# Attention value transposes one slot earlier, the last pair's stages a quarter unit later, and the last two down units with the final norm by token halves

## What is computed

```python
hn = rmsnorm(h, norm1)
q, k, v, g, ... = hn @ W_in                      # one combined projection
a = retention(4 heads);  b = gated_linear_attention(4 heads)
c = band_softmax_attention(8 heads)              # own chunk and 8 before
h = h + concat[a, b, c] @ W_out
h = h + relu(rmsnorm(h, norm2) @ W_up)**2 @ W_down
...
y = rmsnorm(h, final_norm)                       # after the second layer
```

## Time and profile before

| | us |
|---|---|
| median of 3 runs | 1369.89 (1369.73 to 1370.03) |
| profiled execution | 1369.59 |
| its span, first to last instruction | 1367.8 |
| TensorE busy in the span | 1338.8 (98%) |
| VectorE, ScalarE, GpSimd busy | 970.7, 644.5, 118.6 |
| mean granted TensorE clock | 0.994 of full speed |

### The profile page before, as it was taken

The page is one execution under the profiler, slowest core; times in us unless marked ns, Lnnn a source line. Parts: engine busy times, 40 slices in busy tenths (PEclk is TensorE's granted clock), DMA queues, the critical chain, the costliest instruction groups (busy, mean ns, idle before and its releaser), DMA issues. The chain is left out here.

```text
span 1367.8 us, 28726 instructions
## 1 busy us (share of the span) xinstructions
PE 1338.8 (98%) x12206; PEld 1296.8 (95%) x12206; DVE 970.7 (71%) x1480; ACT 644.5 (47%) x1051; POOL 118.6 (9%) x93
## 2 busy tenths in 40 slices
PE   9999999999999999999999999999999999999996
PEld 8999889899999999999998999888999999999995
DVE  6897766778767567666759967767885776756753
ACT  5423555746526337255433345566572462542741
POOL 0000000012020110200200000000211102011011
PEclk9999999999999999999999999999999999999997
DMA  6223333222222223223221223431222232222311
GB/s 232 70 67 102 100 101 120 79 85 86 99 102 78 97 90 108 80 91 109 84 74 49 69 86 124 130 104 63 93 87 100 78 109 93 88 98 93 96 60 66
DMA packets 50639, 127.83 MB, mean 93 GB/s; under 512 B 8400, under 2 KB 17744, under 8 KB 50512
## 3 DMA queue, kind: packets, MB, share of 16 engines
q1 hardware_dynamic: 50224, 125.44, 27.5%
q10 hardware_dynamic: 288, 0.55, 0.1%
HBM read 118.77 MB, written 7.21 MB: 92 GB/s over the span
## 5 line engine op out<-in xcount | busy, mean ns | idle before, releaser
L1685 PE MATMUL PS<-zhi,wlo 128*128 128x272 f32 x1280 | 370.4, 289 | 0.0
L1685 PE MATMUL PS<-zhi,whi 128*128 128x272 f32 x1280 | 368.8, 288 | 0.4 <-DVE wlo L984 0.4
L1685 PE MATMUL PS<-zlo,whi 128*128 128x272 f32 x1280 | 368.3, 288 | 0.0
L539 ACT ACTIVATE whi<-raw 128x1024 fp32r<-128x1024 f32 x136 | 143.7, 1058 | 308.8 <-PE PS L1685 303.9
L1685 PE MATMUL PS<-xhi,whi 128*128 128x272 f32 x896 | 268.9, 300 | 2.3 <-DVE wlo L984 2.2
L1685 PE MATMUL PS<-xhi,wlo 128*128 128x272 f32 x896 | 258.9, 289 | 0.0
L1685 PE MATMUL PS<-xlo,whi 128*128 128x272 f32 x896 | 258.5, 289 | 0.0
L1685 PEld LDWEIGHTS PS<-zhi,whi 128*128 128x128 f32 x1280 | 241.0, 188 | 0.9 <-DVE wlo L984 0.9
L1685 PEld LDWEIGHTS PS<-zlo,whi 128*128 128x128 f32 x1280 | 241.2, 188 | 0.0
L1685 PEld LDWEIGHTS PS<-zhi,wlo 128*128 128x128 f32 x1280 | 240.6, 188 | 0.0
L984 DVE TENSOR_TENSOR wlo<-raw,whi 128x1024 fp32r<-128x1024 f32 x136 | 209.3, 1539 | 39.9 <-ACT whi L539 39.0
(11 more groups left out here) (287 smaller groups left out, 2427.8 us busy)
## 6 DMA issues: line engine op xcount, KB each, us to landing
raw<-in_wu SPq DMA_DIRECT2D x199, 512.0 KB, 3.5
Bh<-in_bias SPq DMA_DIRECT2D x16, 256.0 KB, 4.0
h<-in_x SPq DMA_DIRECT2D x8, 272.0 KB, 6.2
out_k_t<-att_k SPq DMA_DIRECT2D x8, 272.0 KB, 4.4
out_y_t<-y SPq DMA_DIRECT2D x8, 272.0 KB, 2.7
kct<-in_ck SPq DMA_DIRECT2D x8, 256.0 KB, 3.3
cvb<-in_cv SPq DMA_DIRECT2D x8, 256.0 KB, 4.0
out_v_p<-vtk SPq DMA_DIRECT2D x8, 256.0 KB, 2.2
```

The source lines that it names most:

```text
L539: nc.scalar.activation(whi[n % SPL][:, :], raw[n % RAW][:, :], ACT.Copy).then_inc(sems["w_hi"], 1)
L1685: return nc.tensor.matmul(out, lhsT, rhs, start=start, stop=stop, skip_group_check=True)
```

## The change

Three parts.

1. `heads` of pairs 1 to 3 moves from slot (16+3u, 1) to (15+3u, 1), behind `turn_s` of the pair in front. It writes PSUM banks `M0 + 1` and `M0 + 2` where it wrote `M0` and `M0 + 2`.
2. The last pair: TensorE takes `turn 1` ahead of (27, 1), where it took it in the middle of (27, 0), and `pv` and `turn_s` in the middle of (27, 1), where it took them ahead of it. ScalarE's copies of `turn 1` move from slot (27, 0) to (27, 1), and with that behind `gate_out(1)` and `gate_log(2)`; its and VectorE's `pv` steps go behind the last slot's gate work.
3. The end: `d6` and `d7` run as first half of `d6`, first half of `d7`, second half of `d6`, second half of `d7`. VectorE scales and adds both by halves (GpSimd no longer takes part in `d6` and `y`). The norm's sums, root, broadcast and `y` are made for each token half: those of the first half stand on TensorE between the matmuls of the second. The outputs go in eight DMAs of two tiles x 272 tokens; two of the last four are issued by ScalarE's queue.

```diff
-    PE_STEPS[(_b, 1)] = [("heads", _u)]
+    if _u == 0:
+        PE_STEPS[(_b, 1)] = [("heads", _u)]
...
-    PE_STEPS[(_b + 2, 1)] = [("pv", _u), ("turn_s", _u)]
-
-MID = [("back", GLA), ("back", RET), ("turn", 3, 1)]
+    PE_STEPS[(_b + 2, 1)] = [("pv", _u), ("turn_s", _u)] + [("heads", _u + 1)] * (_u < 3)
+
+PE_STEPS[(27, 0)], PE_STEPS[(27, 1)] = [], [("turn", 3, 1), ("pv", 3), ("turn_s", 3)]
+MID = [("back", GLA), ("back", RET), ("pv", 3), ("turn_s", 3)]
...
+ACT_STEPS[(27, 1)], DVE_STEPS[(27, 1)] = [("turn", 3, 1)], []
...
                         if half == 1 and n > GATE:
                             gate_exp(n - GATE - 1)
+                    stage(("pv", 3))
+                    stage(("turn_s", 3))
...
-                for m in range(KC):
-                    if m < YP:
-                        sp.wait_ge(y_pool, m + 1)
-                    else:
-                        sp.wait_ge(y_dve, m - YP + 1)
-                    sp.dma_start(y_t[m, :, :], y[m][:, :]).then_inc(y_out, 16)
+                for a in range(2):
+                    c = slice(a * HT, (a + 1) * HT)
+                    for m in range(0, KC, 2 + 2 * a):
+                        sp.wait_ge(y_dve, a * KC + m + 2)
+                        sp.dma_start(y_t[m:m + 2, :, c].rearrange("m p t -> p m t"), y[:, m:m + 2, c]).then_inc(y_out, 16)
...
+                for a in range(2):
+                    c, o = slice(a * HT, (a + 1) * HT), slice(a * YT, (a + 1) * YT)
+                    for i in range(2):
+                        act.wait_ge(tail_added, 2 * a + i + 1)
+                        squares(KC - 2 + i, L, c)
...
+                for m in (2, 6):
+                    act.wait_ge(y_dve, KC + m + 2)
+                    act.dma_start(y_t[m:m + 2, :, HT:T].rearrange("m p t -> p m t"), y[:, m:m + 2, HT:T]).then_inc(y_out, 16)
...
+                tail_add(0, 0)
+                tail_add(1, 0)
+                tail_square(0)
+                tail_rstd(0)
+                tail_add(0, 1)
+                tail_square(1)
+                tail_y(0, range(6))
+                tail_add(1, 1)
+                tail_y(0, range(6, KC))
+                tail_rstd(1)
+                tail_y(1, range(KC))
...
+                def tail_sums(a):
+
+                    pe.wait_ge(sems["ss_ready"], L * KC + KC - 1 + a)
+                    pe.wait_ge(sems["squared"], L * 2 * KC + KC + 2 * a)
+                    for i in range(YT):
+                        t0, o = a * HT + min(i * P, HT - P), PS[:, M0, a * YT + i:a * YT + i + 1]
+                        mm(o, ssum[:, t0:t0 + P], ones[:, 0:1], True, False)
+                        last = mm(o, nt[1][:, t0:t0 + P], ones[:, 0:1], False, True)
+                    last.then_inc(y_sums, 1)
...
+                begin(d6)
+                tail_products(d6, 0)
+                begin(d7)
+                tail_products(d7, 0)
+                tail_products(d6, 1, all_kc[:4])
+                tail_sums(0)
+                tail_products(d6, 1, all_kc[4:])
+                tail_wide(0)
+                tail_products(d7, 1)
+                tail_sums(1)
+                tail_wide(1)
```

More of the change, by code:

```diff
@@ L34 @@
 NEG = -1e30
-YP = 2
+YT = 3
 WARM = 16
@@ L245, in hybrid_encoder @@
         sm = sb("sm", [P, L * NSM + KC])
-        yv, yl, yr, yn = (sb(n, [P, NT + 1]) for n in ("yv", "yl", "yr", "yn"))
+        yv, yl, yr, yn = (sb(n, [P, 2 * YT]) for n in ("yv", "yl", "yr", "yn"))
         dec = sb("dec", [P, 2, NC + 1])
@@ L312, in hybrid_encoder @@
         assert o + 32 * HT <= nc.sbuf_usable_end
-        y = [at(f"y{m}", [P, T], arena + 4 * T * m) for m in range(KC)]
-        y_rstd = at("y_rstd", [P, T], arena + 4 * T * KC)
+        y = at("y", [P, KC, T], arena)
         PS = ctx.enter_context(nc.psum_tensor("PS", [P, 8, 512], F32))
-        y_by = [PS[:, b:b + 2, :].rearrange("p a b -> p (a b)")[:, 0:T] for b in (M0 + 2, 0)]
         def halves(t):
@@ L333, in hybrid_encoder @@
         x_in = [sem(f"x_in{kc}") for kc in range(KC)]
-        y_sums, y_mean, y_log, y_guess, y_col, y_wide, y_copied, y_scaled, y_dve, y_pool, y_out = (
-            sem(n) for n in ("y_sums", "y_mean", "y_log", "y_guess", "y_col", "y_wide", "y_copied", "y_scaled",
-                             "y_dve", "y_pool", "y_out"))
+        tail_done, tail_added, y_sums, y_mean, y_log, y_guess, y_col, y_wide, y_dve, y_out = (
+            sem(n) for n in ("tail_done", "tail_added", "y_sums", "y_mean", "y_log", "y_guess", "y_col", "y_wide",
+                             "y_dve", "y_out"))
         names = [
@@ L500, in _ @@
                         for m in range(KC):
-                            if g == GROUPS - 1 and m == KC - 1:
+                            if g == GROUPS - 1 and m == KC - (1 if layer + 1 < L else 2):
                                 break
@@ L505, in _ @@
                                 .then_inc(sems["sq_used"], 1)
[L507 to L510, removed]
             @block.scalar
@@ L657, in stage @@
                             s = u % 2
-                            nc.scalar.activation(vtk[s][:, 0:NT, :], PS[:, M0, :].rearrange("p (i c) -> p i c", c=P), ACT.Copy)
+                            nc.scalar.activation(vtk[s][:, 0:NT, :], PS[:, M0 + 1, :].rearrange("p (i c) -> p i c", c=P), ACT.Copy)
                             nc.scalar.activation(vtk[s][0:TS, NT, :], PS[0:TS, M0 + 2, 0:P], ACT.Copy) \
@@ L952, in _ @@
                         next_x(KC - 1)
[L953 to L963, removed]
+                for a in range(2):
[3 more added lines that the diff above has]
+                        squares(KC - 2 + i, L, c)
+                    act.wait_ge(y_mean, a + 1)
+                    nc.scalar.activation(yl[:, o], yv[:, o], ACT.Ln).then_inc(y_log, 1)
+                    act.wait_ge(y_log, a + 1)
+                    nc.scalar.activation(yr[:, o], yl[:, o], ACT.Exp, scale=-0.5).then_inc(y_guess, 1)
+                for m in (2, 6):
+                    act.wait_ge(y_dve, KC + m + 2)
+                    act.dma_start(y_t[m:m + 2, :, HT:T].rearrange("m p t -> p m t"), y[:, m:m + 2, HT:T]).then_inc(y_out, 16)
             @block.vector
@@ L1609, in _ @@
                         for m in range(1, KC):
-                            scaled(m - 1, g)
+                            if m < KC - 1 or g < GROUPS - 1 or layer + 1 < L:
+                                scaled(m - 1, g)
                             if m < KC - 1:
@@ L1636, in _ @@
                         xlo_tile(KC - 2, w0 + NSM, 2 * KC - 1)
-                    add_square(KC - 2, layer + 1)
-                    last_scaled()
-                    if layer + 1 < L:
+                        add_square(KC - 2, layer + 1)
+                        last_scaled()
                         rest(UNITS + 1)
@@ L1642, in _ @@
                         add_square(KC - 1, layer + 1)
-                for a in range(2):
-                    c = slice(a * HT, (a + 1) * HT)
[L1646 to L1661, removed]
+                def tail_add(i, a):
+                    m, c = KC - 2 + i, slice(a * HT, (a + 1) * HT)
+                    dve.wait_ge(tail_done, 2 * a + i + 1)
+                    dve.wait_ge(sems["sq_used"], nth("sq_used", GROUPS * KC + m - 1))
+                    link(nc.vector.tensor_tensor(sq[i][:, c], PS[:, bank(m) + a, 0:HT], r2[:, c], ALU.mult))
+                    nc.vector.tensor_tensor(h[:, m, c], h[:, m, c], sq[i][:, c], ALU.add).then_inc(tail_added, 1)
@@ new lines, in tail_square, with tail_rstd @@
+                def tail_square(a):
+                    c = slice(a * HT, (a + 1) * HT)
+                    dve.wait_ge(sems["squared"], L * 2 * KC + KC - 1 + 2 * a)
+                    dve.wait_ge(sems["ss_ready"], L * KC + KC - 2 + a)
+                    nc.vector.tensor_tensor(ssum[:, c], ssum[:, c], nt[0][:, c], ALU.add).then_inc(sems["ss_ready"], 1)
+                def tail_rstd(a):
+                    o = slice(a * YT, (a + 1) * YT)
+                    dve.wait_ge(y_sums, a + 1)
+                    nc.vector.tensor_scalar(yv[:, o], PS[:, M0, o], 1.0 / D, EPS, ALU.mult, ALU.add).then_inc(y_mean, 1)
+                    dve.wait_ge(y_mean, a + 1)
+                    dve.wait_ge(y_guess, a + 1)
+                    link(nc.vector.tensor_tensor(yl[:, o], yr[:, o], yr[:, o], ALU.mult))
+                    link(nc.vector.tensor_tensor(yl[:, o], yl[:, o], yv[:, o], ALU.mult))
+                    link(nc.vector.tensor_scalar(yl[:, o], yl[:, o], -0.5, 1.5, ALU.mult, ALU.add))
+                    nc.vector.tensor_tensor(yn[:, o], yr[:, o], yl[:, o], ALU.mult).then_inc(y_col, 1)
@@ new lines, in tail_y @@
+                def tail_y(a, tiles):
+                    c = slice(a * HT, (a + 1) * HT)
+                    dve.wait_ge(y_wide, a + 1)
+                    for m in tiles:
+                        dve.wait_ge(tail_added, 4 if a else 2)
+                        nc.vector.scalar_tensor_tensor(y[:, m, c], h[:, m, c], sm[:, WF + m:WF + m + 1],
```

(31 more changed lines are left out.)

5 lines of the change are left out of this document (1 added, 4 removed).

## The result

The changed kernel takes 1372.75 us (median of 20 runs, 1370.62 to 1375.46); the kernel before takes 1369.95 in the same comparison (20 runs, 1369.13 to 1370.53). The ratio is 1.0021, with an interval of 1.0014 to 1.0027: some 0.2% slower, 2.8 us. The single runs now lie 4.8 us apart, where those of before lay 1.4 apart. The execution that was profiled is one of the shorter ones: 1371.06, span 1369.3.

The account below looks back on a forecast made before the run. TensorE was taken to bound the kernel, working 1338.8 of 1367.8 us. Late copies +3.9, clock +2.6 and end -3.5 gave +3.0 on the span; with the offset from span to median, 1372.9 us, range 1367.0 to 1376.0.

Parts of the forecast that it names:

- Late copies: Last pair's pv in each layer waits for ScalarE's PT copies, queued behind gate_log(2): +3.9 us over both layers.
- The wait ahead of `turn 0`: Last pair: the wait for vtk turns into one of about 0.7 us for VectorE to free score banks.
- The clock: TensorE's clock falls behind the long pauses at the last pair's pv: 1.3 us a layer, +2.6 us.
- The deduction of 0.4 us: At each pv pause, 1.3 us taken instead of the bound 1.7, since part of the low stretch may fall into it.
- at both layers: The main forecast's case: the clock goes down behind the last pair's pv in both layers, chance 0.50.
- The premise for the waits of before: Inside the layers of the kernel before, TensorE waits of 1.4 us and less let the clock stay at 1.0.
- the rule that it cites for this term: Trainium skill on TensorE's clock: the slow state is the default and activity releases it; by it both pauses are paid.
- The end: Behind the last matmuls: output work by token halves leaves less open at the finish, -3.5 us, bounds -5 and -0.8.
- the second half's sums: Norm sums on TensorE behind the last unit matmul: 12 records at 0.19 us, ending at 1354.9.
- The clock that holds: Rival: the pv pauses are there but the clock stays, 1370.3 us; clock up at one or both layers, chance 0.32.
- The faster case: Rival: PT is not late at the last pair's pv, 1.3 us gained a layer, 1363.8 us; chance 0.11.
- The output paid by the piece: Rival: output DMAs cost fixed time per piece, so the end gains 0.8 only, 1375.6 us; chance 0.07.

Follow-up runs that it names:

- filler_ahead: Changed kernel plus twelve constant matmuls a layer on TensorE, ahead of both waits for PT before the last pair's pv: 1369.80 us, ratio 1.0000.
- attn_only: Parts 1 and 2 of the change alone, with the end as in the kernel before: 1376.71 us, ratio 1.0051.
- tail_only: Part 3 of the change alone, with attention as in the kernel before: 1365.95 us, ratio 0.9973.
- heads_only: Part 1 alone on the kernel before, heads of pairs 1 to 3 a slot earlier: 1369.74 us, ratio 1.0003.
- copies_first: Changed kernel with ScalarE's copies of turn 1 back in slot (27, 0), ahead of gate_out and gate_log: 1363.51 us, ratio 0.9960.
- last_only: Part 2 alone on the kernel before, the last pair's stages later and ScalarE's copies behind the gates: 1375.75 us, ratio 1.0043.
- copies_first_heads3_back: copies_first with heads of pair 3 back at slot (25, 1), pairs 1 and 2 still moved: 1363.00 us, ratio 0.9955.

## Why the prediction was right, point by point

The forecast was 1372.9 us, and 1372.75 was measured. Its three terms were +3.9, +2.6 and -3.5. The profiles, cut at the two marks, give them one by one:

| kernel | ahead of the first mark, us | first mark to `d5` | `d5` to the end | falls of the clock between the marks |
|---|---|---|---|---|
| before | 52.1 | 1284.0 | 31.8 | 0 |
| changed | 52.4 | 1289.3 | 27.7 | 1 |
| `filler_ahead` | 51.6 | 1287.7 | 28.5 | 0 |
| `attn_only` | 51.6 | 1291.0 | 31.4 | 2 |
| `tail_only` | 51.5 | 1285.2 | 27.6 | 1 |
| `heads_only` | 53.1 | 1284.8 | 31.7 | 0 |
| `copies_first` | 51.5 | 1281.8 | 27.5 | 0 |

**Late copies, +3.9 us.** Right in mechanism and nearly in size: `filler_ahead`, with no fall between the marks, takes 3.7 us more than before there. In the profile after, the copies follow the Ln of `gate_log(2)` directly, and the waits are 2.97 and 3.34 us, where 3.2 and 3.6 stood in the forecast. Its own times gave 3.1 and 3.5 (931.6 less 928.5 in layer 1). TensorE came to `pv` as forecast: 933.75 less the wait and less the 2.26 us by which the mark is later is 928.5. The copies were there 0.1 to 0.2 us sooner (`pv` at 931.5 and, in layer 0, at 263.2), since `heads` delays the chain by 0.4 us and not by 0.55, as `heads_only` shows. `copies_first` is the direct test of the cause.

**The wait ahead of `turn 0`** was said to be 0.7 us and is 1.1. In the frame of before TensorE comes at 917.5, 0.2 us sooner than I had it, and goes on at 918.6, 0.2 later. I had let it go as soon as the last bank was read, at 918.45; the trace names the `mx` read that follows on VectorE. In the changed kernel the 0.4 us are hidden, because TensorE comes to `pv` too early anyway.

**The clock, +2.6 us.** It cost 2.95 us on the median (changed kernel less `filler_ahead`). Here the number came out well in part by luck, since it was built from two steps that were both off. I had two falls at 1.3 us each. A fall behind `pv` costs 1.6 to 1.7: 1.6 by layer 0 of `attn_only`, and the changed kernel takes 1.6 us more between the marks than `filler_ahead`, for one fall. By these an average execution of the changed kernel would have 1.7 to 1.8 falls (an estimate, 2.95 over 1.6 to 1.7). The deduction of 0.4 us for a low stretch that falls into the pause was not borne out, and "at both layers" holds for some executions only: in the profile after the clock fell in layer 1 alone, in `attn_only` and `last_only` in both layers.

The premise for the waits of before, that those of 1.4 us and less leave the clock up, was read from one execution. `tail_only` and `copies_first_heads3_back` each have a fall behind a wait of 1.1 us. And the pause at the start of the kernel, from which the price was taken, is not always followed by a fall either: in `tail_only` it is 2.75 us and the clock stays at 1.00. The single runs of the changed kernel fit falls that come and go: those with a mean clock of 0.995 took 1370.6 to 1371.3 us, those with 0.991 took 1374.6 to 1375.5. What decides whether the clock falls behind a given pause stays open.

The prediction read from the rule that it cites for this term that both pauses are paid. Layer 0 of the changed kernel shows one of 3.34 us that is not, so the rule alone does not give the number of falls.

**The end, -3.5 us.** The mechanism was right, the size was 0.4 us short: 3.9 by `tail_only`. In the profile after, `d5` is read 5.58 us later than before. Less this, the last unit matmul ends at 1356.8 - 5.6 = 1351.2 (forecast 1350.7), the last `tail_add` starts at 1351.5 (1351.2), the eight half tiles of `y` at 1357.6 (1358.0), and the span ends at 1363.7 (1364.3). The term that was mis-sized is the second half's sums: 12 records at 0.19 us, 2.2 in all, for which the profile shows 1.5 at 2.4 GHz. This too depends on the execution: in `filler_ahead` the clock was 0.51 over most of them, and its end took 28.5 us, 0.8 more than that of the changed kernel.

**The rivals.** The clock that holds (1370.3) is what `filler_ahead` makes of the kernel, 1369.8; the lowest single run of the changed kernel is 1370.6. The faster case had the right place: with the copies in time the kernel goes to 1363.5, and I had 1363.8 for it. Its terms were off against each other, 1.3 us a layer where the marks show 1.1, and 3.5 for the end where it is 3.9. It was ruled out for the change as it stands by ScalarE's order alone. The output paid by the piece is out: 272 KB in pieces of 1088 bytes landed in 2.2 us, which is also what the Trainium skill's least transfer for full rate (DMA: Bandwidth & Descriptors, Specifications) let expect.

## What to carry to other kernels

When a consumer on one engine is moved later, look at where its producer's entry ends up in the producer's queue: here a copy that was moved by the same slot came behind 2.7 us of gate work that nobody was waiting for. A wait that is removed ahead of a chain of two other engines isn't saved; it comes back under the next name, unless the chain itself gets shorter. Allow for a fall of the clock behind a pause of TensorE, 1.2 to 1.7 us each here, and expect that it comes in some executions and not in others, behind pauses of 3 us and, in two of the profiles here, behind one of 1.1. Cut profiles at marks that no edit touches: that shows 0.4 us a layer where whole times show nothing. Overlap of the last norm with the last matmuls is worth having; with VectorE's order as it is here, the halves cost without it.

## What I had not expected of the hardware

The same pause in the same place is followed by a fall of the clock in one execution and not in another: the granted clock was 1.00 behind 3.34 us in layer 0 of the changed kernel, and 0.51 in the matching place of `attn_only`. A wait of 1.12 us was followed by one in `tail_only`, a wait of 2.75 us in the same profile was not. Filling a pause with useless matmuls shortened the kernel by 2.95 us. The Trainium skill (TensorE: Matmul & The Clock Gate, Part 1) says that activity releases the slow state. The trace of the changed kernel agrees: in layer 1 TensorE was busy for the whole 3.40 us at a clock of 0.51, and the clock behind them was 1.00. In `filler_ahead` it was at work in place of the pause (11.71 of the 12.00 us from 929 to 941), and the clock was 1.00 there.
